# A fourth seven-product unit in the first half of each FFN, and the softplus moved into the first down projection

## The reference

```python
def swiglu(x, w_gate, w_up, w_down):
    return (jax.nn.silu(x @ w_gate) * (x @ w_up)) @ w_down

h = x + 0.5 * rmsnorm(swiglu(rmsnorm(x, ffn1_pre_g), ffn1_w_gate, ffn1_w_up, ffn1_w_down), ffn1_post_g)
z = rmsnorm(h, mix_pre_g) @ w_in
...
log_a = -8.0 * r * jax.nn.softplus(-lam)      # RG-LRU, one value of lam per channel
a = jnp.exp(log_a)
...
h = h + rmsnorm(concat(y_lru, y_sc) @ w_out, mix_post_g)
h = h + 0.5 * rmsnorm(swiglu(rmsnorm(h, ffn2_pre_g), ffn2_w_gate, ffn2_w_up, ffn2_w_down), ffn2_post_g)
```

## Time and profile before

| | us |
|---|---|
| median of 3 runs | 1730.94 |
| lowest, highest | 1729.77, 1735.61 |
| profiled execution, its own time | 1730.54 |
| its span, first to last instruction | 1728.7 |

### The profile page before, as it was taken

One profiled execution on the slowest core, in us unless ns is written; L12 is line 12 of the kernel. 1 busy time (PEld: TensorE's weight loads), 2 busy tenths in 40 slices (PEclk: granted clock), 3 DMA queues, 4 the chain that ended last, 5 costly groups with the idle time before them and its releaser, 6 DMA issues.

```text
span 1728.7 us, 21174 instructions
## 1 busy us (share of the span) xinstructions
PE 1715.3 (99%) x7708; PEld 1416.3 (82%) x7708; DVE 1471.4 (85%) x1317; ACT 1012.4 (59%) x969; POOL 247.5 (14%) x190
## 2 busy tenths in 40 slices
PE   9999999999999999999999999999999999999998
PEld 7887888888888888788888888888888888888886
DVE  6999999999999878755685558999999999989787
ACT  6665666655656444756654447555656656755454
POOL 4222222222000000100000006122222222000000
PEclk9999999999999999999999999999999999999999
DMA  7788788887767667575565557787888888577665
GB/s 234 233 241 232 227 239 240 233 240 225 230 198 237 211 202 251 180 233 173 166 195 183 185 182 260 206 247 228 243 231 239 237 239 233 192 230 229 207 202 207
DMA packets 150951, 380.26 MB, mean 220 GB/s; under 512 B 12748, under 2 KB 14932, under 8 KB 150100
## 3 DMA queue, kind: packets, MB, share of 16 engines
q1 hardware_dynamic: 134996, 350.33, 61.7%
q0 software_dynamic: 15840, 28.84, 10.6%
q10 hardware_dynamic: 32, 0.01, 0.0%
HBM read 374.94 MB, written 4.19 MB: 219 GB/s over the span
## 4 chain that ended last, share of the span: by engine, by line
PE 94%; DVE 3%; DMA 1%; ACT 1%; issue 0%; POOL 0%; DVEq 0%; SPq 0%; ACTq 0%
PE ps L1816 22%; PE ps L1818 22%; PE ps L1817 22%; PE ps L1705 8%; PE ps L1707 8%; PE ps L1706 8%; DMA u_raw<-in_ffn_w_gate 1%; PE ps L1811 1%; DVE u_lo L1270 1%; DVE w_lo L1132 1%; PE ps L2026 1%; PE ps L1747 0%; PE ps L2038 0%; DVE tsum L1285 0%; PE ps L1737 0%
## 5 line engine op out<-in xcount | busy, mean ns | idle before, releaser
L856 ACT CAST u_hi<-u_raw 128x2048 fp32r<-128x2048 f32 x160 | 306.1, 1913 | 184.1 <-DMA u_raw<-in_ffn_w_up 90.3
L1270 DVE TENSOR_TENSOR u_lo<-u_raw,u_hi 128x2048 fp32r<-128x2048 f32 x142 | 325.2, 2290 | 11.0 <-ACT u_hi L856 0.8
L1132 DVE TENSOR_TENSOR w_lo<-raw,w_hi 128x1024 fp32r<-128x1024 f32 x156 | 196.7, 1268 | 130.5 <-ACT w_hi L744 128.3
L744 ACT CAST w_hi<-raw 128x1024 fp32r<-128x1024 f32 x160 | 166.7, 1051 | 136.5 <-PE ps L1707 112.7
L1816 PE MATMUL ps<-u_hi,xT_hi 128*128 128x512 f32 x576 | 224.5, 390 | 0.0
L1818 PE MATMUL ps<-u_hi,xT_lo 128*128 128x512 f32 x576 | 224.4, 390 | 0.0
L1021 ACT CAST d_hi<-d_raw 128x2048 fp32r<-128x2048 f32 x80 | 152.9, 1913 | 121.9 <-DVE d_raw L1494 61.0
L1817 PE MATMUL ps<-u_lo,xT_hi 128*128 128x512 f32 x576 | 224.1, 389 | 0.0
L863 ACT CAST t_hi<-tsum 128x1536 fp32r<-128x1536 f32 x96 | 142.6, 1485 | 97.1 <-DVE tsum L1285 95.5
L1487 DVE TENSOR_TENSOR d_lo<-d_raw,d_hi 128x2048 fp32r<-128x2048 f32 x80 | 182.9, 2288 | 15.3 <-ACT d_hi L1021 11.8
L1705 PE MATMUL ps<-w_hi,xT_hi 128*128 128x512 f32 x448 | 178.1, 397 | 2.7 <-DVE xT_lo L1173 2.4
(11 more groups left out here) (212 smaller groups left out, 3203.5 us busy)
## 6 DMA issues: line engine op xcount, KB each, us to landing
d_raw<-in_ffn_w_down SPq DMA_DIRECT2D x50, 1024.0 KB, 5.3
raw<-in_w_in SPq DMA_DIRECT2D x80, 512.0 KB, 3.7
u_raw<-in_ffn_w_gate SPq DMA_DIRECT2D x34, 1024.0 KB, 5.3
u_raw<-in_ffn_w_up SPq DMA_DIRECT2D x30, 1024.0 KB, 5.1
u_raw<-in_ffn_w_up SPq DMA_DIRECT2D x100, 256.0 KB, 4.3
u_raw<-in_ffn_w_up SPq DMA_DIRECT2D x50, 512.0 KB, 3.8
u_raw<-in_ffn_w_gate SPq DMA_DIRECT2D x92, 256.0 KB, 4.0
u_raw<-in_ffn_w_gate SPq DMA_DIRECT2D x46, 512.0 KB, 3.7
```

The source lines that it names most:

```text
L744: sc.copy(w_hi[:, s], raw[:, s]).then_inc(hi_ready, 1)
L856: sc.copy(unit(u_hi, p), unit(u_raw, p)).then_inc(unit_hi, 1)
L1132: ve.tensor_tensor(w_lo[:, s], raw[:, s], w_hi[:, s].bitcast(f32), ALU.subtract).then_inc(lo_ready, 1)
L1270: ve.tensor_tensor(unit(u_lo, p), unit(u_raw, p), unit(u_hi, p).bitcast(f32), ALU.subtract).then_inc(unit_lo, 1)
```

## The change

Unit 3 of c = 0 becomes a seven. VectorE runs sums_of_unit_3 ahead of half_sums(3), then half_lo(3), the lo parts of forms 7 to 9, and sums_lo(3); ScalarE takes the hi parts of those forms ahead of sums_hi(3). TensorE waits for all ten forms before unit 3 of c = 0, where it waited before unit 3 of c = 1. The number of sevens per FFN goes from 48 to 49, so that the sum buffers alternate the other way round from c = 1 on. The copy of the constants stays in the first up chunk as "constants". The two instructions of "lambda" go in front of the sums of the first seven of the second down group, the sigmoid behind ScalarE's cast of that unit, and "series" and "end" behind the first and the second `split` of the last eight down groups.

```diff
-    SEVEN = [(2, 4, 6)] + [(0, 2, 3, 4, 6)] * (HALVES - 1)
+    SEVEN = [(2, 3, 4, 6)] + [(0, 2, 3, 4, 6)] * (HALVES - 1)
...
                 for j in range(GP, 2 * GP):
                     if j < GP + 4:
                         block_squares(2 * f, j - GP)
-                    if f == 0 and j == GP + 6:
-                        act.wait_ge(lam_neg, 1)
-                        sc.activation(soft[:, 1], soft[:, 0], ACT.Sigmoid).then_inc(lam_sig, 1)
...
                 half_hi(f, q, 3)
-                if seven(q, 3):
-                    sums_hi(f, q, 3)
+                if q[1] == 0:
+                    form_hi_of(f, 7, 8, 9)
+                sums_hi(f, q, 3)
                 half_hi(f, q, 4)
                 sums_hi(f, q, 4)
                 half_hi(f, q, 5)
-                if q[1] == 0:
-                    form_hi_of(f, 7, 8, 9)
...
                 down_hi(f, GF + 3)
+                if f == 0:
+                    act.wait_ge(lam_neg, 1)
+                    sc.activation(soft[:, 1], soft[:, 0], ACT.Sigmoid).then_inc(lam_sig, 1)
...
-                    if f == 0 and j in (GP + 5, GP + 7):
-                        softplus(("lambda", "series")[j == GP + 7])
+                    if f == 0 and j == GP + 5:
+                        softplus("constants")
...
-                if seven(q, 3):
-                    half_sums(f, q, 3)
-                half_lo(f, q, 3)
-                if seven(q, 3):
-                    sums_lo(f, q, 3)
                 if c == 0:
                     sums_of_unit_3(f)
+                half_sums(f, q, 3)
+                half_lo(f, q, 3)
+                if c == 0:
+                    form_lo_of(f, 7, 8, 9)
+                sums_lo(f, q, 3)
                 half_sums(f, q, 4)
                 half_lo(f, q, 4)
                 sums_lo(f, q, 4)
                 half_lo(f, q, 5)
...
-                if c == 0:
-                    form_lo_of(f, 7, 8, 9)
...
                 half_steps(f, (0, 0))
-                if f == 0:
-                    softplus("end")
...
                 down_lo(f, GF + 2)
+                if f == 0:
+                    softplus("lambda")
...
                 for j in range(SLOTS):
                     split(last, j)
+                    if f == 0 and j < 2:
+                        softplus(("series", "end")[j])
...
                 if c == 0 and p < 3:
                     pe.wait_ge(form_lo, NF * f + (2, 4, 7)[p])
-                elif c == 1 and p == 3:
+                elif c == 0 and p == 3:
                     pe.wait_ge(form_lo, NF * (f + 1))
```

More of the change, by code:

```diff
@@ L121, in hybrid_block_kernel @@
     EVAC = 7
-    assert FC == 2 * PAIRS + 1 and HALVES == 2 + 2 * TURN and NS % 2 == turn_sevens % 2 == 0
+    assert FC == 2 * PAIRS + 1 and HALVES == 2 + 2 * TURN and turn_sevens % 2 == 0
     DU = GF - SLOTS
@@ L1549, in softplus @@
                 s, q, neg, w, w2 = (soft[:, n] for n in range(5))
-                if what == "lambda":
+                if what == "constants":
                     dve.wait_ge(small_xp, 2)
                     ve.tensor_copy(cst[:, KD:], bank(7, NB)).then_inc(cst_ready, 1)
+                elif what == "lambda":
                     dve.wait_ge(cst_ready, 2)
```

## The result

The changed kernel takes 1734.2 us in the median (from 1731.41), the kernel before 1730.93 in the same comparison, 22 runs of each. One of after's, 1903.92 us at a mean granted clock of 0.851, is left out of the ratio; the other 21 end at 1738.34. The ratio is 1.0015, its 95% interval 1.0009 to 1.0022: 2.6 us slower, 1.6 to 3.8 (the two medians lie 3.3 apart, inside that interval). The forecast was 1733.0, 2.1 over the median shown, and "within 0.3%". So the change, which takes six matmuls out, costs time. The profiled execution of after took 1735.28 us by its own time, with a span of 1733.5.

What follows compares the result with a forecast made beforehand. TensorE was taken to set the time nearly everywhere. 1730.54 us - 1.36 for matmuls + 2 x 1.76 of waits gave 1732.7, on the median 1733.1; 1733.0 was given, range 1729.2 to 1736.5.

Steps and rivals of the forecast that it cites:

- The price of a matmul, and six fewer: TensorE, unit 3 of both FFNs: three matmuls fewer each at 0.227 us, -1.36 us in all, 7702 instead of 7708.
- VectorE's added work and the waits: Ahead of unit 4, first halves: 4.52 us added against 3.49 of slack, waits of 1.76 us per FFN including handoff.
- How the wait is split: Second FFN's first half: TensorE waits 0.7 to 0.8 us before unit 3 and about 1.0 before unit 4.
- Unit 3's transfer: GpSimd's accumulating transfer lands at 1086.1, at the longest 1088.4, against 1089.5 where half_sums(3) stands: hidden, 0 us.
- The softplus in its new place: First down projection: VectorE's idle 4.14 and 3.30 us cover the moved pieces, cost 0 or 0.1 us.
- another table load: Rival, down projection: Square after the sigmoid makes ScalarE load a table again, 1.28 us, total 1733 to 1734.3; chance 0.05.
- leaves work that no matmul waited for: 0: First chunk: taking away the softplus's 2.44 us of VectorE, a 1.28 us table load and 0.2 of ScalarE gains nothing.
- The delay neither grows nor is won back: Rest of each FFN after unit 4: the net delay of +1.08 us per FFN stands.
- holes in later halves that weren't there: Sign against the forecast: it is wrong if TensorE shows new holes in later halves; no size given.
- Full cover: Rival: VectorE reaches unit 4 in time, so only the removed matmuls show, 1729.5 us; chance 0.18 with half cover.
- Late transfer: Rival: unit 3's accumulating transfer lands after 1089.5 and delays VectorE and TensorE; at 1092.5, 1739 us; chance 0.06.
- The delay grows: Rival: VectorE's lag meets a later wait for `u_lo`, 1.0 us more in each FFN, 1735 us; chance 0.13.

Runs made afterwards that it cites:

- e8: The changed kernel once more, unchanged, for a second profile: 1733.15 us, ratio 1.0014 to the kernel before.
- e12: e2 with only the softplus's four "end" operations moved behind the second split of the last down groups: 1733.47 us, ratio 1.0006 to the kernel before.
- e2: The changed kernel with the softplus back in its old places, so only unit 3 becomes a seven: 1735.62 us, ratio 1.0028 to the kernel before.
- e9: The kernel before once more, unchanged, for a second profile: one execution, 1734.08 us.
- e1: The kernel before with only the softplus moved into the first down projection, no fourth seven: 1731.02 us, ratio 1.0000.
- e6: The kernel before with four added 128x512 VectorE additions (2.9 us) ahead of half_sums(4) in each FFN's first half: 1735.04 us, ratio 1.0025.
- e7: As e6, but six added VectorE additions (4.3 us) on the kernel before: 1737.65 us, ratio 1.0036.
- e10: The four additions of e6 on top of e1's moved softplus: 1730.71 us, ratio 0.9992 to the kernel before.
- e11: The six additions of e7 on top of e1's moved softplus: 1732.03 us, ratio 0.9998 to the kernel before.
- e5: The changed kernel with unit 3's sums and the low parts of forms 7 to 9 (first FFN also 4, 5) made earlier: 1729.22 us, ratio 0.9994 to before.
- e13: e5 once more, unchanged: 1729.78 us, ratio 0.9987 to the kernel before.

## Why the prediction was right, and what in it was not

**The price of a matmul, and six fewer.** Right: 7702, and the sum above works with 0.227.

**VectorE's added work and the waits.** Forecast: 4.52 us added against 3.49 of slack, waits of 1.76 per FFN. From `sums_of_unit_3` to unit 4's remainder it is 1098.62 - 1088.96 = 9.66 us in after, and was 1093.77 - 1088.45 = 5.32: 4.34 added. The waits are 1.49 in the first FFN and 1.74 in the second, in e8 1.48 and 1.78. Of the 0.27 that the first is short of the forecast, 0.18 is the smaller addition. In the second it was made up by VectorE's own lateness of 0.3 (next point). What the series' going gave is 0.30 us of its 2.44, by e12's 1.79 where it stays; forecast 0.35.

**How the wait is split.** Missed: 1.15 before unit 3 and 0.59 before unit 4, not 0.75 and 1.0. Unit 3 waits for the last form. VectorE began `sums_of_unit_3` at 1088.96, 0.51 later than the step had it. TensorE shares 0.23 of that: unit 0 begins at 1078.34, in before at 1078.11. The other 0.3 is VectorE's own, and no step of the prediction has it: unit 1's remainder begins 2.49 us behind unit 0's first matmul, in before 2.20. It isn't chance. The profiles of e8, e2 and e12, which have the seven with its steps where the change puts them, show 2.49 to 2.50; those of e9, e1, e6, e7, e10 and e11, without the seven, 2.20 or 2.21. ScalarE's cast of unit 1, which that remainder waits for, begins 0.55 behind the matmul in the first and 0.25 or 0.26 in the others. Why, no run here shows; in the first FFN it isn't so (2.20 in after and e8). Together with the handoff, 0.15 and not 0.05, it makes the 0.4 by which the hole before unit 3 was too small in the forecast. In the total it was hidden by the smaller addition: the 1.74 for 1.76 forecast is in part luck. Unit 4 begins 22.62 us behind unit 0, in before 21.44: 1.18 later, forecast 1.08.

**Unit 3's transfer.** Hidden, as forecast, with far more room. GpSimd's transfers for units 2 and 3 in after, answering:

```profile
1074.09 0.90 POOL L687 DMA_DIRECT2D u_raw<-in_ffn_w_gate  x1 [2.24 <-DMA u_raw<-in_ffn_w_gate]
1076.60 0.88 POOL L687 DMA_DIRECT2D u_raw<-in_ffn_w_gate  x1 [1.60 <-DMA u_raw<-in_ffn_w_gate]
```

Unit 3's is issued 2.5 us behind unit 2's. With the longest landing time of the earlier trace rows, 7.1, it is there at 1083.7, with the longest in after, 7.5, at 1084.1, and it is wanted at 1090.03. I had put 8.4 us between SyncE's issue and GpSimd's, from one row.

**The softplus in its new place.** Right. VectorE of after in the down projection, answering and the last of the earlier trace rows:

```profile
609.63 0.69 DVE L1501 TENSOR_TENSOR dsum<-d_raw 128x512 f32<-128x512 f32 x1 [3.07 <-PE ps L1818]
...
688.80 3.94 DVE L1131 TENSOR_TENSOR w_lo<-raw,w_hi 128x1024 fp32r<-128x1024 f32 x3 [0.23 <-ACT w_hi L744]
```

The idle time of 4.14 has shrunk to 3.07, and the one of 3.30 to 0.23. TensorE has no new hole at either; e1 at 1.0000 says the same. The rival *another table load* is refuted. ScalarE of after, the sigmoid's load, the Square and the next load:

```profile
598.95 1.28 ACT L980 ACT_TABLE_LOAD   x1
...
694.94 0.59 ACT L753 ACTIVATE act_g<-ps 128x512 f32<-128x512 f32 x1
...
696.21 1.28 ACT L773 ACT_TABLE_LOAD   x1
```

The Square at 694.94 runs without a load since the sigmoid's at 598.95; the next load is for the square root.

**The softplus gone from its old place.** This is the step that was wrong: "leaves work that no matmul waited for: 0". It looked only at the pieces in front of the FFN. The four operations of "end" stand between two halves, ahead of the bank sums and 0.02 us in front of GpSimd's instruction. In an execution like e9's they cost TensorE a hole of 3.44 us (its last start 100.80, the next 104.47), and the six slower starts behind it some 1.4 more. How often before meets this can be read only indirectly, by the mean granted clock of an execution: e7's profile, where the clock is low for some 7 us behind the hole, has 0.997. e9's has 0.998, a value that two executions of after have without the meeting, so only 0.997 is counted. Of before's 91 executions beside the experiments five have that, and they take 1734.9 to 1737.7 us. Of e6's twelve five have it, of e7's six one (the other five have 0.998), of e2's eleven none (two have 0.998). Of the 114 of kernels with "end" moved (after among them) none has. The count is a lower bound, since e6's and e9's profiles show the hold at 0.999 and 0.998. So the term was small against before as it is, by an estimate 0.3 us or more from five in 91 at some 5 us each, and some 2 to 4 us against the seven without the move: e2's 1.0028 minus after's 1.0015, and e2's minus e12's 1.0006. With a different order of the edits, this would have been the term that decided.

**The delay neither grows nor is won back.** Supported on the average, not in each execution. In the profile of after the holes of the later halves sum to 1.07 us in the first FFN and 3.57 in the second; in e8's, the same kernel, to 0.85 and 0.18, and its own time is 1730.67 against 1735.28. The holes of after begin with late transfers. The second idle time below is put down to "issue", but GpSimd's transfer for that unit, issued at 1128.11, landed at 1134.43, 0.08 ahead of its end. VectorE and TensorE of after:

```profile
1114.49 0.69 DVE L1282 TENSOR_TENSOR tsum<-u_raw 128x512 f32<-128x512 f32 x1 [1.58 <-DMA u_raw<-in_ffn_w_up]
...
1134.51 0.69 DVE L1282 TENSOR_TENSOR tsum<-u_raw 128x512 f32<-128x512 f32 x1 [2.23 <-issue]
```

```profile
1138.91 0.50 PE L1816 MATMUL ps<-u_hi,xf 128*128 128x512 f32 x1 [1.41 <-DVE u_lo L1269]
```

Before has such holes too (1.62 and 0.65 in its profile). By my own test, "holes in later halves that weren't there", the forecast would have been called wrong from one profile; the test was badly put, since one execution can't tell these holes from the change. What the two executions share, the holes in c = 0, is 3.23 and 3.26 us; minus 1.36 that is +1.9, and the ratio says 2.6 (1.6 to 3.8). Whether the remaining 0.7 is real stays open.

**The rivals.** *Full cover* fell: both holes are there. In e5 and e13, where VectorE's queue gets its cover back, the time is that of full cover (1729.22 and 1729.78, forecast 1729.5). The prediction had a rule of the Trainium skill speak for it, "Perfetto Trace Analysis", section Identifying the Most-Contended Engine. That was misread: the section doesn't take the share of matmul records as TensorE's measure and names, beside the arithmetic done, the busy share of weight loads. By that share TensorE has 82% and VectorE 85%, so it named VectorE, and in after work added to VectorE's queue cost more than the matmuls gave. *Late transfer* fell, as above. *The delay grows* by 2 us isn't borne out by e8.

## What to carry to other kernels

Taking work off the engine with the highest share pays only as far as the second engine's queue, at that very place, has slack for what the trick adds; compute it as the distance from the last needed step to the matmul, and if it is short, move the added steps earlier in the same queue, where the slack is, before giving the trick up. Small operations on VectorE need not be small where GpSimd works: look what starts within a few tenths of a microsecond beside them, because a delay elsewhere can push them into it. When a change has two parts, measure each alone and look whether the sum of them is the whole; here 1.0000 and 1.0028 against 1.0015 pointed at the mechanism that no profile of the change showed.

## What the hardware showed that I had not expected

- **A 128x8 operation that lasts as long as GpSimd's.** VectorE's operations of 0.17 us take 2.25 to 2.31 when they meet GpSimd's 2.4 us subtraction of 128x1024, twice in a row (e6, e7, e9). VectorE's own subtractions from PSUM beside it keep 0.68.
- **Executions differ by who comes first.** Before passes the meeting by 0.02 us in one execution and not in another. The same happens with the splits in the second up chunk, between 1064 and 1079 us: the last two take 2.31 us each beside GpSimd's forms in eleven of fourteen profiles, 1.21 in three. In those three GpSimd's last form takes about 2.35 in place of 1.62: there it is GpSimd that is held. Before has 1.21 in one and 2.31 in the other (e9), so it is not of the change.
- **TensorE's clock after a hole.** In e9, after 3.4 us without a matmul, the granted clock of the next stretch is 0.50, its level of 1.2 GHz, and the matmuls start 0.43 us apart. In e7, after its hole of 3.77 us at the same place, it is 0.50 too, from 107 to 112. After e6's hole at 103.53, of 3.38 us, it stays at 1.00. Windows of e9 (stretch, length, busy PE, PEld, DVE, ACT, POOL, then the granted clock, DMA share, GB/s) and of e6:

```profile
104.00:106.00 2.00, 1.53 (x4) 1.25 (x5) 2.00 (x4) 0.00 (x0) 0.88 (x1) 0.50 0.81 260
106.00:108.00 2.00, 2.00 (x8) 1.57 (x7) 1.97 (x4) 0.00 (x0) 0.00 (x0) 0.67 0.75 125
```

```profile
103.50:105.00 1.50, 1.47 (x6) 1.05 (x6) 1.50 (x3) 0.00 (x0) 0.70 (x1) 1.00 0.67 217
```

Why two of the holes cost the clock and the third doesn't, no run here shows.
